# First expert layer of a PEER block: products with u's high parts ahead of a separate wait for the low parts, and the first two tiles of u split behind the query's weights

## What is computed

```python
qy = (xb @ w_query).reshape(n_tok, PEER_HEADS, 2, half)
s1 = einsum('nhd,hkd->nhk', qy[:, :, 0], sub_keys_1); s2 = ...   # 8 heads, 128 keys a side
v1, i1 = top_k(s1, 16); v2, i2 = top_k(s2, 16)
top_s, pos = top_k(v1[..., :, None] + v2[..., None, :], 16)       # 16 experts of each head
u, vv = expert_u[eidx], expert_v[eidx]
act = gelu(einsum('nhkd,nd->nhk', u, xb))
y = einsum('nhk,nhkd->nd', softmax(top_s) * act, vv)
```

## Time and profile before

| | us |
|---|---|
| median of three runs | 1742.41 (1742.08 to 1749.11) |
| profiled execution | 1741.93 |
| its span | 1739.9 |
| PE busy | 1647.5 (95%) |
| DVE busy | 1365.6 (78%) |
| ACT busy | 682.2 (39%) |
| POOL busy | 552.7 (32%) |
| mean granted clock of PE | 0.978 of full |

### The profile page before, as it was taken

How to read it: one execution, slowest core, us unless ns; L and a number is a source line. 1 busy time by engine, 2 the same in 40 slices (tenths; PEclk the granted TensorE clock), 3 DMA queues, 4 the chain that set the end, 5 groups by cost and what they waited for, 6 DMA issues and landing times.

```text
span 1739.9 us, 27680 instructions
## 1 busy us (share of the span) xinstructions
PE 1647.5 (95%) x9711; PEld 1413.0 (81%) x9711; DVE 1365.6 (78%) x2501; ACT 682.2 (39%) x1068; POOL 552.7 (32%) x393
## 2 busy tenths in 40 slices
PE   6998887968999999999899999999999999999998
PEld 4876575545777999999899999999888888888886
DVE  6744577777641589999989998966888889888887
ACT  5474223245332343433344444433333333333334
POOL 5000000004530467877732332323323233322220
PEclk9999997879999999999999999999999999999999
DMA  3321010000323468888778888999999999999995
GB/s 127 108 73 57 2 39 1 25 24 31 103 76 130 128 189 283 283 280 256 253 246 322 316 314 297 325 345 362 389 385 373 370 392 385 382 371 357 337 367 211
DMA packets 149143, 405.00 MB, mean 233 GB/s; under 512 B 14100, under 2 KB 71700, under 8 KB 145592
## 3 DMA queue, kind: packets, MB, share of 16 engines
q1 hardware_dynamic: 108728, 244.38, 41.6%
q0 software_dynamic: 36864, 134.23, 20.2%
q10 hardware_dynamic: 3456, 25.17, 3.6%
HBM read 351.29 MB, written 52.44 MB: 232 GB/s over the span
## 4 chain that ended last, share of the span: by engine, by line
PE 51%; DVE 11%; DMA 2%; issue 2%; ACT 1%; POOL 1%; DVEq 0%; SPq 0%; ACTq 0%
PE bank L1536 9%; PE bank L1538 9%; PE bank L1537 9%; PE bank L2057 7%; PE bank L2059 6%; PE bank L2058 6%; PE bank L2079 4%; DVE own_waste L1841 3%; DMA front<-active_scratch 2%; DMA h<-u_rows_dram,own_experts 1%; POOL rt_u_lo L1803 1%; DVE rt_num L1863 1%; DVE rt_num L1856 1%; DVE back L1892 1%; DVE rt_work L1857 0%
## 5 line engine op out<-in xcount | busy, mean ns | idle before, releaser
L2057 PE MATMUL bank<-hi_parts,rt_u_hi 128*128 128x384 f32 x1024 | 352.2, 344 | 11.6 <-POOL rt_u_lo L1803 10.7
L2059 PE MATMUL bank<-hi_parts,rt_u_lo 128*128 128x384 f32 x1024 | 344.1, 336 | 0.0
L2058 PE MATMUL bank<-lo_parts,rt_u_hi 128*128 128x384 f32 x1024 | 344.0, 336 | 0.0
L1536 PE MATMUL bank<-rt_u_hi,rt_w_hi 128*128 128x512 f32 x768 | 299.3, 390 | 2.0 <-DVE rt_w_lo L1452 1.9
L1538 PE MATMUL bank<-rt_u_lo,rt_w_hi 128*128 128x512 f32 x768 | 298.8, 389 | 0.0
L1537 PE MATMUL bank<-rt_u_hi,rt_w_lo 128*128 128x512 f32 x768 | 298.8, 389 | 0.0
L1755 ACT ACTIVATE rt_u_hi<-raw 128x1024 fp32r<-128x1024 f32 x128 | 135.6, 1060 | 370.4 <-PE bank L2059 314.8
L1396 ACT ACTIVATE rt_u_hi<-raw 128x1024 fp32r<-128x1024 f32 x128 | 135.9, 1061 | 316.9 <-PE bank L1538 284.5
L2108 POOL DMA_INDIRECT h<-u_rows_dram,own_experts x128 | 169.9, 1327 | 261.2 <-DVE own_waste L1841 248.4
L2114 POOL DMA_INDIRECT qy<-v_dram,own_experts x128 | 132.6, 1036 | 348.7 <-DVE qy L1470 342.8
L1803 POOL TENSOR_TENSOR rt_u_lo<-raw,rt_u_hi 128x1024 fp32r<-128x1024 f32 x68 | 167.8, 2468 | 138.0 <-ACT rt_u_hi L1755 136.9
(11 more groups left out here) (353 smaller groups left out, 2681.9 us busy)
## 6 DMA issues: line engine op xcount, KB each, us to landing
raw<-u_dram SPq DMA_DIRECT2D x128, 512.0 KB
raw<-v_dram SPq DMA_DIRECT2D x128, 512.0 KB
active_scratch<-rt_act SPq DMA_DIRECT2D x128, 192.0 KB
gates_scratch<-front ACTq DMA_DIRECT2D x12, 1024.0 KB
gates_scratch<-back ACTq DMA_DIRECT2D x12, 1024.0 KB, 8.2
front<-gates_scratch SPq DMA_DIRECT2D x8, 1536.0 KB
front<-active_scratch SPq DMA_DIRECT2D x64, 192.0 KB
back<-active_scratch SPq DMA_DIRECT2D x64, 192.0 KB
```

The lines of the kernel that those rows point to most:

```text
L1536: mm(bank, w_hi[:, j, block], v_hi[:, j, cols], start=False, stop=False)
L2057: mm(bank, u_hi[:, j % 2, cols], hi[:, c, 0:TD], start=c == 0, stop=False)
L2058: mm(bank, u_hi[:, j % 2, cols], lo[:, c, 0:TD], start=False, stop=False)
L2059: last = mm(bank, u_lo[:, j % 2, cols], hi[:, c, 0:TD], start=False, stop=c == DC - 1)
```

## The change

Three things. PE no longer waits for a tile's low part at its start: it waits for the high part, does the 16 products with `u_hi`, then waits for the low part and does the eight with `u_lo`. The splits of tiles 0 and 1 move from the start of `route_stage` to the end of `Tail`: ACT's two copies go between the stores of query items 13 and 14, the two subtractions go from POOL to the end of DVE's part. For this `u_hi` and `u_lo` get the place of `proj`'s first 16 KB a partition, which nothing uses by then, and `u_high` and `u_low` are made outside of the stages, so that the barrier doesn't clear them.

```diff
@@ Tail.scalar
             store(i - 2 - self.OUT)
+        for e in range(2):
+            act.wait_ge(self.u_in[e], 16)
+            f(self.u_hi[:, e, :], self.u[:, e, :], ACT.Copy).then_inc(self.u_high, 1)
         for q in (2 * PH - 2, 2 * PH - 1):
             store(q)
@@ Tail.vector
             w_rest(i)
+        for e in range(2):
+            dve.wait_ge(self.u_high, e + 1)
+            tt(self.u_lo[:, e, :], self.u[:, e, :], self.u_hi[:, e, :].bitcast(F32), ALU.subtract).then_inc(self.u_low, 1)
@@ route_stage
-    u_high, u_low, u_low_late, first, active = (
-        t.sem("rt_" + k) for k in ("u_high", "u_low", "u_low_late", "first", "active"))
+    u_high, u_low = ahead["u_high"], ahead["u_low"]
+    u_low_late, first, active = (t.sem("rt_" + k) for k in ("u_low_late", "first", "active"))
-        u_hi, u_lo = sb("u_hi", [P, 2, D], F32R), sb("u_lo", [P, 2, D], F32R)
@@ scalar, step
-                    act.wait_ge(ld_u[j % 4], 16 * (turn(phase, i, j) + 1))
                     fresh = head and phase == 0 and j < 2
                     if not fresh:
+                        act.wait_ge(ld_u[j % 4], 16 * (turn(phase, i, j) + 1))
                         act.wait_ge(first, e - 1)
-                    a(u_hi[:, j % 2, :], raw[:, j % 4, :], ACT.Copy).then_inc(u_high, 1)
-                    if not fresh:
+                        a(u_hi[:, j % 2, :], raw[:, j % 4, :], ACT.Copy).then_inc(u_high, 1)
@@ gpsimd
-                for e in range(BODY + 1):
+                for e in range(2, BODY + 1):
                     low(e)
@@ tensor, step
-                    low_wait(pe, phase, i, j)
+                    pe.wait_ge(u_high, e + 1)
                     if not (head and phase == 0 and j < 2):
                         pe.wait_ge(active, e - 1)
                     bank = t.bank[j % 2][:, 0:TD]
+                    chunk = [slice(c * P, (c + 1) * P) for c in range(DC)]
                     for c in range(DC):
-                        cols = slice(c * P, (c + 1) * P)
-                        mm(bank, u_hi[:, j % 2, cols], hi[:, c, 0:TD], start=c == 0, stop=False)
-                        mm(bank, u_hi[:, j % 2, cols], lo[:, c, 0:TD], start=False, stop=False)
-                        last = mm(bank, u_lo[:, j % 2, cols], hi[:, c, 0:TD], start=False, stop=c == DC - 1)
+                        mm(bank, u_hi[:, j % 2, chunk[c]], hi[:, c, 0:TD], start=c == 0, stop=False)
+                        mm(bank, u_hi[:, j % 2, chunk[c]], lo[:, c, 0:TD], start=False, stop=False)
+                    low_wait(pe, phase, i, j)
+                    for c in range(DC):
+                        last = mm(bank, u_lo[:, j % 2, chunk[c]], hi[:, c, 0:TD], start=False, stop=c == DC - 1)
                     last.then_inc(first, 1)
@@ build
+            place = nc.sbuf_base
             proj = inner.enter_context(nc.sbuf_tensor("proj", [P, NPROJ, PAD + T + 1], F32))
+            u_parts = nc.alloc_sbuf_tensor_at("rt_u_parts", [P, 4, D], F32R, offset=place)
+            u_hi, u_lo = u_parts[:, 0:2, :], u_parts[:, 2:4, :]
...
         with ExitStack() as peer:
+            peer.enter_context(nc.sbuf_tensor("u_parts_place", [P, 4, D], F32))
```

More of the change, by code:

```diff
@@ L385, with __init__ @@
     OUT, LEAD, N = DC, 4, DC + 2 * PH
-    def __init__(self, t, x, mix, hi, lo, x_hi, x_lo, qy, raw, whi, wlo, inv, w_out, w_query):
+    def __init__(self, t, x, mix, hi, lo, x_hi, x_lo, qy, raw, whi, wlo, inv, w_out, w_query, u, u_hi, u_lo, ahead):
         self.t, self.x, self.mix, self.hi, self.lo, self.x_hi, self.x_lo = t, x, mix, hi, lo, x_hi, x_lo
@@ L390, in __init__ @@
         self.w_out, self.w_query = w_out, w_query
+        self.u, self.u_hi, self.u_lo, self.u_in = u, u_hi, u_lo, ahead["u"]
+        self.u_high, self.u_low = ahead["u_high"], ahead["u_low"]
         self.loaded = [t.sem(f"tail_loaded{s}") for s in range(2)]
@@ L1557, in value_layer, with route_stage @@
     return sync, split, follow, scalar, gpsimd, clear, vector, tensor
-def route_stage(t, x, qy, y, hi, lo, raw, front, back, u_d, gates_d, active_d, v_d, eidx, w_own, ahead, last_d, out_d):
+def route_stage(t, x, qy, y, hi, lo, raw, front, back, u_hi, u_lo, u_d, gates_d, active_d, v_d, eidx, w_own, ahead, last_d, out_d):
     nc = t.nc
@@ L2143, in build @@
         ahead = {"u": [nc.alloc_semaphore(name=f"rt_u_loaded{i}") for i in range(4)],
-                 "keys": nc.alloc_semaphore(name="rt_keys")}
+                 "keys": nc.alloc_semaphore(name="rt_keys"),
+                 "u_high": nc.alloc_semaphore(name="rt_u_high"), "u_low": nc.alloc_semaphore(name="rt_u_low")}
         def first_tiles(sp):
@@ L2156, in build @@
             w_parts = [conv_parts[:, k * H:(k + 1) * H, :].rearrange("p (s c) t -> p s (c t)", s=2) for k in (1, 2)]
-            tail = Tail(t, x, y, hi, lo, rough_hi, rough_lo, qy, weights, *w_parts, proj[:, 8, 0:T], a["w_out"], a["w_query"])
+            tail = Tail(t, x, y, hi, lo, rough_hi, rough_lo, qy, weights, *w_parts, proj[:, 8, 0:T], a["w_out"], a["w_query"],
+                        raw, u_hi, u_lo, ahead)
             mixer_stage(t, proj, conv, y, hi_rows, lo_rows, qy, raw_rows, front_rows, tail,
@@ L2169, in build @@
             ahead["act"] = [half[:, spread + j * TD:spread + (j + 1) * TD] for half in (front, back) for j in range(2)]
-            route_stage(t, x, qy, y, hi, lo, raw, front, back, a["u"], a["gates"], a["active"], a["v"], eidx, w_own, ahead,
+            route_stage(t, x, qy, y, hi, lo, raw, front, back, u_hi, u_lo, a["u"], a["gates"], a["active"], a["v"], eidx, w_own, ahead,
                         a["final_rows"], a["out"])
```

## The result

The changed kernel takes 1728.44 us in the median of 9 runs (1724.88 to 1734.48). Nine runs of the kernel before gave 1741.03 (1732.56 to 1749.11). The ratio is 0.9934, 95% interval 0.9915 to 0.9952: 8 to 15 us faster. The forecast was 1734.5 in a range of 1730.0 to 1739.0: the sign is right, the size is short, and the measured time lies outside the range. The profiled execution took 1727.22 us, its span 1725.4.

A forecast was written before the change was run, and what follows sets the result against it. TensorE was taken to bound the layer when unhindered, VectorE's chain in its middle. Terms 3.2 + 1.1 + 0 + 2.8 + 0.8 = 7.9 us off 1741.93 gave 1734.0, or 1734.5 for the median, range 1730.0 to 1739.0.

The forecast's parts named there:

- The start: Layer start, tile 0: moving the splits of tiles 0 and 1 into the query's tail saves 3.2 us, bounds 1.1 to 4.7.
- a lost start: Layer start: tile, copy or store slips into the barrier, so the moved splits do not help; 1737.7 us, chance 0.08.
- a clock that stays up: Layer start: the clock does not fall after the barrier's gap, giving 4.7 us instead of 3.2; 1733.0 us, chance 0.06.
- Early stalls: From 568 to 638, where TensorE leads: short stalls on low parts go entirely, saving 1.1 us.
- VectorE's way, 698 to 863: Mid-layer, where VectorE paces: TensorE's gains at its stalls only bring it earlier to the next late low part; 0 us.
- one or two holds less: VectorE's chain shortens by one or two holds of 2.1 us each: 1732.4 or 1730.3 us, chance 0.20.
- I see no reason for one sign: 0 in the sum: VectorE's chain: holds may grow or shrink, so they count 0, with plus or minus two holds in the range.
- Tile 65: Low part 4.3 us earlier, wait still about 5 us, clock still falls, but 8 products left instead of 24: 2.8 us saved.
- the signs of a wrong forecast: Slow mid-tile steps, late ScalarE stores, a new VectorE or TensorE wait at 870 to 905, or an end that moved much less.
- The room of 2.2 us: After tile 65: low parts of tiles 66 and 67 come early enough, 2.2 us to spare, so nothing takes back the 2.8.
- 1068.73: Late layer, where TensorE paces: its one stall on a low part goes, saving 0.8 us, or 0 if one-hots are late.
- The slower rival: Every tile: the second wait breaks TensorE's stream even when satisfied, 0.11 us times 128 tiles; 1748.6 us, chance 0.04.

The follow-up runs named there:

- order_only: The kernel before with only the new order of products and the separate wait for the low part, splits not moved: 1728.26 us, ratio 0.9944 to the kernel before.
- small_low: The changed kernel with GpSimd's subtractions of tiles 2 to 67 cut from 1024 to 32 columns: 1723.15 us, ratio 0.9905 to the kernel before.
- splits_only: The changed kernel with the old order of products and the old wait, only the splits of tiles 0 and 1 moved: 1739.68 us, ratio 1.0002.
- reordered_old_wait: The changed kernel with the wait for the low part back at each tile's start, products in the new order: 1735.85 us, ratio 0.9982.
- after_again: The changed kernel run once more without an edit, for a second profile: 1729.15 us, ratio 0.9947 to the kernel before.
- seven_more_waits: The changed kernel with the high-part wait repeated before seven of each tile's eight chunks, 896 more satisfied waits: 1728.15 us, ratio 0.9931.
- slots_early: The changed kernel with the transposes of the last block's slots put between tile 71's high and low products: 1726.77 us, ratio 0.9921.
- low_first: The changed kernel with GpSimd's subtractions of tiles 65 to 67 issued ahead of the gather that held them: 1727.85 us, ratio 0.9928.
- old_wait_32_to_63: The changed kernel with the low-part wait back at the start of tiles 32 to 63 only: 1731.99 us, ratio 0.9946 to the kernel before.

## Why the prediction was short, point by point

**The start: 3.2 forecast, 3.20 measured**, with the clock's fall behind the barrier and its return after 3.6 us as taken over from the gap at 493.3. The rivals of a lost start and of a clock that stays up fall: the splits were in time, and the clock did fall. But the credit was wrong. The part put all 3.2 under the moved splits and priced their loss at 3.2; order_only shows that the new order alone gives 2.75 of it. The step that failed is that the two parts were costed one after the other, without asking what the second does to the first one's stall. The text had the 2.8 us that the order gives and the 2.4 us of the subtraction, and never set them side by side at tile 0. The Trainium skill's rule on the clock ("TensorE: Matmul & The Clock Gate", HAM oscillation) made 4.7 us of this term; the trace disagrees, with its fall to 0.50 behind 2.25 us of idle time.

**Early stalls: 1.1 forecast, 1.4 measured** at dot 11. Right in kind.

**VectorE's way, 698 to 863: 0 forecast, 3.1 measured.** This is the largest miss. The mechanism was in the text as a rival (one or two holds less, 0.20): PE ahead moves ScalarE's copy, that moves GpSimd's subtraction against VectorE's list, and other instructions meet it. Taken instruction by instruction, the two traces differ by over 0.5 us at seven places between the dots: five stretches are shorter, by 0.7 to 2.1, and two are longer, by 2.4 and 2.2. The rows below show one of the five, before and after. Before, GpSimd starts a subtraction just as VectorE starts its five adds behind a dot, and the adds last 2.85 us (GpSimd, then VectorE):

```profile
834.56 2.39 POOL L1803 TENSOR_TENSOR rt_u_lo<-raw,rt_u_hi 128x1024 fp32r<-128x1024 f32 x1 [1.92 <-ACT rt_u_hi L1755]
834.84 2.85 DVE L1875 TENSOR_TENSOR rt_cand<-rt_val 128x128 f32<-128x128 f32 x5
```

After, the subtraction starts ahead of the dot and ends at 830.06, and the same adds last 1.28:

```profile
827.66 2.40 POOL L1810 TENSOR_TENSOR rt_u_parts<-raw,rt_u_parts 128x1024 fp32r<-128x1024 f32 x1 [0.88 <-ACT rt_u_parts L1763]
829.52 1.28 DVE L1882 TENSOR_TENSOR rt_cand<-rt_val 128x128 f32<-128x128 f32 x5
```

In small_low these adds last 0.88. In both rows above they end 0.74 behind the end of the subtraction (836.95 and 830.06): they stand until it is done, so a hold is as long as what is left of the subtraction, here 1.97 before and 0.40 after. The forecast's fixed 2.1 us a hold is the long case.

What failed is the step "I see no reason for one sign: 0 in the sum". The size stood within the two holds that the range allowed, and the runs show no rule for the sign: that the change gained here and didn't lose is luck as far as they tell. Against the kernel after, the kernel with the old wait in tiles 32 to 63 differs at 13 places, by 0.6 to 2.4 us either way, for a total of 162.05, and the one with the new wait there at four, for 161.07. The traces of before, splits_only and reordered_old_wait agree at every place within 0.5 us; so do those of after, after_again and seven_more_waits. But order_only comes to 160.39 with 12 places changed, and slots_early, whose edit lies behind this stretch, to 160.68 with seven. So the total of 160.4 to 160.8 stands in five traces, while its make-up changes even without an edit there. That it comes from the phase between two instruction lists fits all of this; why three such patterns add up to the same total isn't shown, and the term would have to be measured in any other kernel. That GpSimd's subtraction is the cause of the holds is shown (small_low, and by one moved instruction low_first); that the adds waited for something shared is the reading of the rows. It fits the Trainium skill ("SBUF — State Buffer", Who interferes with whom), by which a VectorE instruction with two inputs in SBUF can be kept waiting for the whole of a GpSimd instruction that reads SBUF. The held casts have one input; what they wait for isn't shown here.

**Tile 65: 2.8 forecast, 4.24 measured.** "The wait is still about 5 us and the clock still falls" failed in both halves, for a reason that lies in the term above. The low part came 7.7 us earlier and not 4.3, so the wait was 2.57 and not 5. The sixteen products that no longer stand behind the wait give 16 x 0.174 = 2.8, as forecast. In this trace the clock stayed up, which gives about 2.2 us more: before, 867 to 871 ran at 0.50 and 871 to 873 at 0.67, in all 15 products at 0.32 instead of 0.174. And 0.72 is lost to one-hots that are now late: 2.8 + 2.2 - 0.7 = 4.3. That wait, between 870 and 905, was named among the signs of a wrong forecast. The room of 2.2 us had been worked out for GpSimd's low parts of tiles 66 and 67 alone; the one-hots, the next thing VectorE owes TensorE, weren't in the list. In the repeat the clock fell, the one-hots were in time, and the piece was worth 2.3 (24.74 - 22.47).

One reading of the text was off without bearing on its sum: it has TensorE stall four times between 698 and 863, where the trace of before has three such stalls on low parts, at 762.99, 791.29 and 837.00.

**1068.73: 0.8 forecast, nothing gained.** The stall on the low part went and a wait of 0.66 for the one-hots took its place at 1056.11. The text had this as "0 if the one-hots are as late"; in this trace they are. In order_only they are not: TensorE has no wait there, and from the placing to the end the layer gains 0.7.

**The slower rival**, a price on each wait, is ruled out by 896 more waits.

The sum: 3.2 + 1.4 + 3.1 + 4.2 - 0.1 = 11.8 against 7.9 forecast. By the medians the miss is larger than these 3.9 us: 1.4 more is the kernel before, which took 1742.41 in the three runs that the forecast started from and 1741.03 in nine. The interval of the ratio, put in times, is 1726 to 1733, so it reaches into the range; the marks show the two wrong terms where the medians alone would not. The range's lower end, 1730.0, allowed for two holds, but not for what a shorter way of VectorE does at tile 65: a shorter wait, and with it a clock that may stay up. The two surprises have one cause, and the range had treated the second as fixed.

Not shown: why the shorter way comes with the new wait in every pattern of holds, and what decides whether the clock falls after a stall of 2.6 us.

## What to carry to other kernels

When a change has two parts that attack the same stall, cost each of them alone and both together: here the second alone made the layer 11.45 us shorter and the first alone 2.3, for 11.83 together. Waiting for an operand in the middle of a group of products instead of at its head was free where the wait was satisfied, and where it wasn't it took up to the 2.8 us of the products ahead of it off the stall. Where two engines hold each other up, a shift of 2 us in one changes the other's length by up to 2.4 us per hold, the length of the instruction that holds, and no sign could be read off beforehand here: give such a term a wide range, carry it through every later term that depends on it, and list all that the next stage waits for, not only the operand that was late before. An edit that moves a holding instruction can lose its gain to a new hold, as low_first did.

## What the runs showed of the hardware that was not expected

Stalls of 2.57 or 2.58 us before tile 65 occurred in five traces with the low wait in its new place (after, after_again, order_only, seven_more_waits, slots_early). In four the granted clock stayed at 2.4 GHz, in one it fell to 1.2 GHz for some 6 us. Behind the barrier's shorter gap, 2.25 us, it fell in all thirteen traces, and in old_wait_32_to_63 it fell in mid-layer after 2.30 us. It fell after the stalls of 4.92 and 5.35, and not after those of 1.80 and 1.82 near the same place as the 2.30. The length of a gap alone doesn't tell it. The Trainium skill ("TensorE: Matmul & The Clock Gate", Part 1: The HAM clock gate) says of the slow products at a kernel's start that one kernel shows different numbers of them from run to run; here a stall in mid-kernel does the like.

Of VectorE's 155.0 busy us in a way of 160.8, 17.9 went away when GpSimd's subtractions were cut short, though both engines look merely busy in the page: a held instruction is drawn as a long one, and only its minimum beside its maximum (226 to 2374 ns) gives it away.
